# RWKV's chunk inverse: its 16x16 diagonal blocks go to VectorE, through a DRAM scratch

## The reference

```python
def step(S, inp):
    r_t, w_t, k_t, v_t, kk_t, a_t = inp
    sa = jnp.einsum("bhvk,bhk->bhv", S, -kk_t)
    S = (S * w_t[:, :, None, :]
         + sa[..., None] * (kk_t * a_t)[:, :, None, :]
         + v_t[..., None] * k_t[:, :, None, :])
    return S, jnp.einsum("bhvk,bhk->bhv", S, r_t)
```

## Time and profile before

| | |
|---|---|
| three timed runs | 3728.26, 3730.78, 3735.71 us |
| median | 3730.78 us |
| the profiled execution's own time | 3736.72 us |
| its span, first to last instruction | 3734.7 us |
| mixers of both layers | about 60 to 2400 us |
| TensorE, VectorE, ScalarE busy | 95%, 36%, 19% of the span |
| mean granted TensorE clock | 0.97 |

### The profile page before, as it was taken

The page is one execution under the profiler, slowest core; times in us unless marked ns, Lnnn a source line. Parts: engine busy times, 40 slices in busy tenths (PEclk is TensorE's granted clock), DMA queues, the critical chain, the costliest instruction groups (busy, mean ns, idle before and its releaser), DMA issues.

```text
span 3734.7 us, 43111 instructions
## 1 busy us (share of the span) xinstructions
PE 3535.5 (95%) x18508; PEld 2956.0 (79%) x18508; DVE 1335.7 (36%) x2779; ACT 720.5 (19%) x1360; POOL 43.5 (1%) x51
## 2 busy tenths in 40 slices
PE   7997999998999999999999999899989988997999
PEld 6997988998987898898898898686658747855684
DVE  3546546537410463655645531100130012015100
ACT  2223222313100232322313210100010011002100
POOL 0000000000000000000000000000000000000000
PEclk9998999999999999998999999999989989997999
DMA  4112122112124321211212122444434423431343
GB/s 183 57 68 71 68 71 79 57 71 91 68 105 150 121 68 68 94 68 49 80 68 84 67 91 102 142 152 153 147 102 139 154 99 124 147 126 68 113 151 108
DMA packets 53117, 375.55 MB, mean 101 GB/s; under 512 B 6049, under 2 KB 6177, under 8 KB 9025
## 3 DMA queue, kind: packets, MB, share of 16 engines
q1 hardware_dynamic: 51376, 368.01, 28.4%
q0 software_dynamic: 1552, 4.79, 0.4%
HBM read 371.72 MB, written 1.05 MB: 100 GB/s over the span
## 4 chain that ended last, share of the span: by engine, by line
PE 90%; DVE 7%; ACT 1%; issue 1%; DMA 1%; SPq 0%; ACTq 0%; DVEq 0%
PE bank L418 42%; PE bank L1635 11%; PE bank L1572 6%; PE bank L435 5%; PE bank L721 5%; PE bank L743 4%; PE bank L732 4%; PE bank L1194 1%; DVE rw_score L998 1%; PE bank L456 1%; PE bank L660 1%; PE bank L1458 1%; PE bank L772 1%; PE bank L708 1%; PE bank L756 1%
## 5 line engine op out<-in xcount | busy, mean ns | idle before, releaser
L418 PE MATMUL bank<-h_features,weight_ring 128*128 128x256 f32 x7072 | 1594.4, 383 | 16.6 <-DMA weight_ring<-in_w_in 9.7
L418 PEld LDWEIGHTS bank<-h_features,weight_ring 128*128 128x128 f32 x7072 | 1335.0, 191 | 200.8 <-issue 13.5
L1635 PE MATMUL bank<-weight_ring,ff_act 128*128 128x512 f32 x704 | 303.1, 592 | 4.7 <-DVE ff_act L1718 4.7
L1635 PEld LDWEIGHTS bank<-weight_ring,ff_act 128*128 128x128 f32 x704 | 133.4, 190 | 172.7 <-issue 166.5
L1718 DVE TENSOR_TENSOR ff_act<-ff_silu,bank 128x256 f32<-128x256 f32 x88 | 37.1, 421 | 577.2 <-ACT ff_silu L1709 577.2
L721 PE MATMUL bank<-rw_bm,rw_score 128*128 128x64 f32 x1536 | 206.5, 278 | 7.2 <-DVE rw_bm L1023 3.7
L721 PEld LDWEIGHTS bank<-rw_bm,rw_score 128*128 128x128 f32 x1536 | 194.7, 196 | 13.7 <-issue 3.4
L435 PE MATMUL bank<-weight_ring,h_features 128*128 128x256 f32 (+2 forms) x896 | 202.5, 375 | 2.0 <-DVE h_features L501 2.0
L743 PE MATMUL bank<-rw_ex,rw_sig 128*128 128x64 f32 x1536 | 203.6, 276 | 0.0
L1023 DVE COPY_PREDICATED rw_bm<-mask_constants,bank 128x256 f32<-128x256 uint32 x160 | 78.6, 491 | 330.8 <-PE bank L732 330.4
L743 PEld LDWEIGHTS bank<-rw_ex,rw_sig 128*128 128x128 f32 x1536 | 191.6, 194 | 1.4
(11 more groups left out here) (420 smaller groups left out, 3592.3 us busy)
## 6 DMA issues: line engine op xcount, KB each, us to landing
weight_ring<-in_w_in SPq DMA_DIRECT2D x146, 1024.0 KB, 4.9
weight_ring<-in_f00w SPq DMA_DIRECT2D x33, 1024.0 KB, 4.9
weight_ring<-in_f01w SPq DMA_DIRECT2D x33, 1024.0 KB, 4.8
weight_ring<-in_f10w SPq DMA_DIRECT2D x33, 1024.0 KB, 4.9
weight_ring<-in_f11w SPq DMA_DIRECT2D x33, 1024.0 KB, 4.9
weight_ring<-in_w_b SPq DMA_DIRECT2D x16, 1024.0 KB, 5.0
weight_ring<-in_w_out SPq DMA_DIRECT2D x16, 1024.0 KB, 5.2
weight_ring<-in_conv_in SPq DMA_DIRECT2D x10, 1024.0 KB, 4.8
```

What stands on the lines that cost most here:

```text
L418: m = e.matmul(bank[:, j, :], w[:, k, j * P:(j + 1) * P], x[:, k, :], start=k == 0, stop=k == kt - 1, skip_group_check=True)
L1635: m = e.matmul(banks[i], src[:, k0 + k, t * P:(t + 1) * P], w[:, k, s * 512:(s + 1) * 512], start=k0 + k == 0, stop=k0 + k == k_tiles - 1, ...
```

## The change

The levels 2, 4 and 8 of the doubling and the "first" products leave TensorE. In their place a unit does this, for both chunks and all four heads at once:

- TensorE makes the a-scores of both chunks first (four banks, two products each), and VectorE masks them into R.scored_a. The kd-scores follow in each step, into R.scored_k;
- ScalarE's queue stores slot 0 of each chunk in a DRAM scratch (`scratch_rows`: 128 partitions x 4 heads, runs of 512 B), waits, and loads the 64 diagonal blocks of 16x16 back with one block on each of 64 partitions (`scratch_blocks`: 64 blocks x 16 rows, runs of 64 B);
- VectorE inverts them in place (`block_inverse_dve`): 4x4 blocks by substitution, then two doublings by multiply and reduce (`product_dve`), and the transposed copy;
- ScalarE's queue stores the inverse and its transpose in two more scratches, and loads each chunk's x and xT from them before the step's first level. The zeros off the blocks come from the scratches, which POOL clears once at the start (`clear_scratch_pool`).

A chunk has 8 diagonal blocks of a head; two chunks and four heads make the 64. On VectorE's queue the masks of scored_k stand behind the inverse. The loads of step 1 are issued when w of step 0 is done, behind ScalarE's copies of tok. The orders of both mixer layers are written anew for TensorE, VectorE, ScalarE and SP. The masks first0 and first1 are gone from the constants.

```diff
     ("mixers0", "tensor"):
-        "H2 R20 H2 R5 H12 R9 H R3 H R4 H R4 H3 R4 B R3 B H R B R3 B R2 H2 R2 B R2 B R4 H2 R8 B R3 B2 R3 H2 R3 B R "
...
+        "H2 R20 H2 R5 H12 R6 H6 B4 R2 B3 R H R3 B2 R B R5 H2 R2 B R2 B R4 H2 R4 B2 R3 B R4 H2 R3 B R2 B R2 H2 R2 "
...
-RW_LEVELS = (2, 4, 8, 16, 32, 64)
+RW_LEVELS = (16, 32, 64)
+BLOCK = 16
+HEAD_STRIDE = P // BLOCK * (BLOCK * P + BLOCK)
...
     R.state = R("state", 2, P)
-    R.score = R("score", 4, 4, P)
+    R.scored_a, R.scored_k = R("scored_a", TT, 4, 2, P), R("scored_k", 4, 2, P)
     R.tot, R.mid, R.phi = R("tot", 4), R("mid", 4), R("phi", 2)
     R.mean, R.var = R("mean", 8), R("var", 8)
     R.prod, R.x, R.xT = (z.rearrange("p n (c s) -> p (n c) s", c=TT) for z in (R.sig, R.bm, R.ex))
+    blocks = TT * 4 * P // BLOCK
+    R.blk, R.inv, R.inv_mid, R.inv_tmp = (flat(z)[0:blocks, a:b] for z, a, b in (
+        (R.sig, 0, 272), (R.bm, 0, 272), (R.bm, 272, 336), (R.ex, 0, 512)))
...
+def scratch_rows(t, c):
+    heads = t[c * 4 * HEAD_STRIDE:(c + 1) * 4 * HEAD_STRIDE].rearrange("(h z) -> h z", h=4)
+    return heads[:, 0:P * P].rearrange("h (s t) -> s h t", s=P)
+def scratch_blocks(t):
+    step = BLOCK * P + BLOCK
+    return t.rearrange("(n z) -> n z", z=step)[:, 0:BLOCK * P].rearrange("n (s t) -> n s t", s=BLOCK)[:, :, 0:BLOCK]
+def block_rows(z):
+    return z[:, 0:BLOCK * BLOCK].rearrange("p (s t) -> p s t", s=BLOCK)
+def diagonal(z, n):
+    step = n * BLOCK + n
+    return z[:, 0:BLOCK // n * step].rearrange("p (b z) -> p b z", z=step)[:, :, 0:n * BLOCK].rearrange(
+        "p b (s t) -> p b s t", s=n)[:, :, :, 0:n]
+def product_dve(e, S, tmp, left, right, outs):
+    dve, n = S.dve, left[0].shape[1]
+    w = tmp[:, 0:len(left) * n ** 3].rearrange("p (b c t k) -> p b c t k", b=len(left), c=n, t=n)
+    for b, (x, y) in enumerate(zip(left, right)):
+        shape = [x.shape[0], n, n, n]
+        e.tensor_tensor(w[:, b], x.rearrange("p k t -> p t k").unsqueeze(1).to_broadcast(shape),
+                        y.unsqueeze(2).to_broadcast(shape), ALU.mult).then_inc(*dve.up())
+    e.wait_ge(*dve.now())
+    for b, out in enumerate(outs):
+        e.tensor_reduce(out, w[:, b], AX.X, ALU.add).then_inc(*dve.up())
+    e.wait_ge(*dve.now())
+def block_inverse_dve(e, g, l, q, d):
+    S, R = g.rw, g.R
+    dve, blk, inv, tmp, mid = S.dve, R.blk, R.inv, R.inv_tmp, R.inv_mid
+    e.memset(inv[:, 0:BLOCK * BLOCK], 0.0).then_inc(*dve.up())
+    e.wait_ge(*dve.now())
+    e.memset(inv[:, 0:BLOCK * BLOCK].rearrange("p (s t) -> p s t", s=BLOCK)[:, 0:1, 0:1], 1.0).then_inc(*dve.up())
+    e.memset(inv[:, 17:17 * BLOCK].rearrange("p (s z) -> p s z", z=17)[:, :, 0:1], 1.0).then_inc(*dve.up())
+    yield
+    e.wait_ge(g.rw_blocks_sem, 16 * ((4 * l + q) * 2 + d + 1))
+    e.wait_ge(*dve.now())
+    b4, i4 = diagonal(blk, 4), diagonal(inv, 4)
+    first, second = (0, 1) if d == 0 else (3, 2)
+    e.tensor_copy(i4[:, :, first, second:second + 1], b4[:, :, first, second:second + 1]).then_inc(*dve.up())
+    e.wait_ge(*dve.now())
+    for i in (2, 3):
+        t, lo = (i, 0) if d == 0 else (3 - i, 4 - i)
+        rows = slice(lo, lo + i)
+        shape = [blk.shape[0], 4, i, i]
+        w = tmp[:, 0:4 * i * i].rearrange("p (b c s) -> p b c s", b=4, c=i)
+        e.tensor_tensor(w, b4[:, :, rows, t].unsqueeze(2).to_broadcast(shape), i4[:, :, rows, rows], ALU.mult
+                        ).then_inc(*dve.up())
+        e.wait_ge(*dve.now())
+        e.tensor_reduce(i4[:, :, rows, t], w, AX.X, ALU.add).then_inc(*dve.up())
+        e.wait_ge(*dve.now())
+    for n in (4, 8):
+        lo, hi = (slice(0, n), slice(n, 2 * n)) if d == 0 else (slice(n, 2 * n), slice(0, n))
+        pairs_of = range(BLOCK // (2 * n))
+        b, x = diagonal(blk, 2 * n), diagonal(inv, 2 * n)
+        m = [mid[:, i * n * n:(i + 1) * n * n].rearrange("p (c k) -> p c k", c=n) for i in pairs_of]
+        product_dve(e, S, tmp, [b[:, i, lo, hi] for i in pairs_of], [x[:, i, lo, lo] for i in pairs_of], m)
+        product_dve(e, S, tmp, [x[:, i, hi, hi] for i in pairs_of], m, [x[:, i, lo, hi] for i in pairs_of])
+    e.tensor_copy(block_rows(tmp), block_rows(inv).rearrange("p c t -> p t c")).then_inc(*dve.up("inverse", l, q, d))
...
+            for c in (0, 1) if d == 0 else (1, 0):
+                for par in range(2):
+                    yield
+                    rows = slice(64 * par, 64 * par + 64)
+                    bank = pairs(g.banks.take(S, "scored_a", l, q, d, c, par))
+                    for free in g.banks.free("scored_a", l, q, d, c, par):
+                        e.wait_ge(*free)
+                    if par == 0:
+                        e.wait_ge(*dve.at("ops", l, q, d))
+                    for n in range(2):
+                        m = e.matmul(bank[:, n, :], R.a[rows, n, c * P:(c + 1) * P],
+                                     R.kr[rows, n, c, :, :].rearrange("p s t -> p (s t)"), start=True, stop=True,
+                                     skip_group_check=True)
+                    m.then_inc(*pe.up("scored_a", l, q, d, c, par))
+
             for step, c in enumerate((0, 1) if d == 0 else (1, 0)):
                 W = (l, q, d, step)
                 cs = slice(c * P, (c + 1) * P)
-                for h in range(4):
-                    n, rows = h // 2, slice(64 * (h % 2), 64 * (h % 2) + 64)
-                    pair = R.kr[rows, n, c, :, :].rearrange("p s t -> p (s t)")
-                    yield
-                    bank = g.banks.take(S, "score", *W, h)
-                    for free in g.banks.free("score", *W, h):
-                        e.wait_ge(*free)
-                    if h == 0:
-                        e.wait_ge(*dve.at("ops", l, q, d))
-                    e.matmul(bank[:, 0:T], R.a[rows, n, cs], pair, start=True, stop=True, skip_group_check=True)
-                    e.matmul(bank[:, T:2 * T], R.kd[rows, n, cs], pair, start=True, stop=True,
-                             skip_group_check=True).then_inc(*pe.up("score", *W, h))
-                    if h % 2 == 1:
-                        yield
-
                 for par in range(2):
                     yield
                     rows = slice(64 * par, 64 * par + 64)
-                    bank = g.banks.take(S, "first", *W, par)
-                    for free in g.banks.free("first", *W, par):
+                    bank = pairs(g.banks.take(S, "scored_k", *W, par))
+                    for free in g.banks.free("scored_k", *W, par):
                         e.wait_ge(*free)
                     for n in range(2):
-                        m = e.matmul(bank[:, n * P:(n + 1) * P], R.kr[rows, n, c, 0, :], R.a[rows, n, cs], start=True,
-                                     stop=True, skip_group_check=True)
-                    m.then_inc(*pe.up("first", *W, par))
-                yield
+                        m = e.matmul(bank[:, n, :], R.kd[rows, n, cs],
+                                     R.kr[rows, n, c, :, :].rearrange("p s t -> p (s t)"), start=True, stop=True,
+                                     skip_group_check=True)
+                    m.then_inc(*pe.up("scored_k", *W, par))
...
-                    e.wait_ge(*dve.at(*(("xT", *W, 1) if lv == 2 else ("x", *W, lv // 2))))
+                    if lv == BLOCK:
+                        e.wait_ge(g.rw_inverse_sem, 32 * (((4 * l + q) * 2 + d) * 2 + step + 1))
+                    else:
+                        e.wait_ge(*dve.at("x", *W, lv // 2))
...
+            unit = (4 * l + q) * 2 + d
+            for c in (0, 1) if d == 0 else (1, 0):
+                yield
+                e.wait_ge(*dve.at("scored_a", l, q, d, c, 1))
+                if unit:
+                    e.wait_ge(g.rw_blocks_sem, 16 * unit)
+                e.dma_start(scratch_rows(g.scores_scratch, c), R.scored_a[:, c, :, 0, :]).then_inc(g.rw_scores_sem, 16)
+            yield
+            e.wait_ge(g.rw_scores_sem, 32 * (unit + 1))
+            e.dma_start(block_rows(R.blk), scratch_blocks(g.scores_scratch)).then_inc(g.rw_blocks_sem, 16)
+            yield
+            e.wait_ge(*dve.at("inverse", l, q, d))
+            e.wait_ge(g.rw_zeros_sem, 32)
+            if unit:
+                e.wait_ge(g.rw_inverse_sem, 64 * unit)
+            e.dma_start(scratch_blocks(g.x_scratch), block_rows(R.inv_tmp)).then_inc(g.rw_stored_sem, 16)
+            e.dma_start(scratch_blocks(g.xT_scratch), block_rows(R.inv)).then_inc(g.rw_stored_sem, 16)
+
             for step, c in enumerate((0, 1) if d == 0 else (1, 0)):
+                W = (l, q, d, step)
                 yield
-                W = (l, q, d, step)
+                if step == 0:
+                    e.wait_ge(g.rw_stored_sem, 32 * (unit + 1))
+                else:
+                    e.wait_ge(*pe.at("w", l, q, d, 0))
+                e.dma_start(R.x, scratch_rows(g.x_scratch, c)).then_inc(g.rw_inverse_sem, 16)
+                e.dma_start(R.xT, scratch_rows(g.xT_scratch, c)).then_inc(g.rw_inverse_sem, 16)
+                yield
...
```

(70 more changed lines are left out.)

27 lines of the change are left out of this document (16 added, 11 removed), and 100 rows, old and new, of the table ORDER.

## The result

The median of four runs is 3561.69 us (3554.92 to 3565.18), beside 3729.55 us of four runs of the kernel before on the same chip: a ratio of 0.9545, with a 95% interval of 0.9527 to 0.9563. The forecast was 3530 us, the range 3435 to 3790. The profiled execution took 3560.88 us, its span is 3558.8 us, 175.9 less than before; by the prediction's sum it should have been 200.9 less.

The account below looks back on a forecast made before the run. The prediction took TensorE's work to bound the kernel: 3736.7 - 348 (removed work) + 114 (gates) + 5 (step 1) + 2 (zeroing) + 26 (clock) = 3536, with the median 6 us lower: 3530 us; range 3435 to 3790.

Parts of the forecast that it names:

- What leaves TensorE: In the mixers: three levels' matmuls save 303.6 us, the "first" products 38.2 plus 5.9 idle before them, 348 in all.
- Only as long as the fixed order still keeps TensorE fed: In the mixers: condition on work taken off TensorE being worth its full price; no size given.
- Price of a DMA leg: Path's transfers: 1.8 us fixed, 42 ns per KB, and f = 25 ns for each packet, one packet per contiguous piece.
- read-modify-write: Stores of 64 B pieces: if each read and wrote 512 B, 135 us more, about 3675; supports the dear-transfers rival.
- Price of the inverse: VectorE's block inverse: 6.2 us a unit, 99 us over all units, about what VectorE lost.
- Two gates: TensorE waits before step 0's rhs (16.0 us path) and level 16 (10.5): less cover, 114 us idle over two layers.
- Step 1: Loads of x and xT land after 6.4 us against 5.6 to 11.0 us of cover: 5 us in all.
- they are late by the same gaps: Other mixers' work queued behind the path's waits, and TensorE's tokens behind rhs, is late by the gates' gaps.
- Clock: Idle TensorE loses granted clock: four long gaps at 4 us, some ten shorter at 1, 26 us in all.
- Short runs are dear: Rival, chance 0.24: short pieces between SBUF and DRAM cost far more; with f = 70 ns a packet, 3810 us.
- The path is hidden: Rival, chance 0.19: with f = 5 ns a packet most gaps are covered, 3445 us.
- The waits hold H and B as well: Rival, chance 0.09: ScalarE's DMA waits delay the other mixers' streams H and B; 100 us added, 3630 us.

Follow-up runs that it names:

- b_drop: The kernel before with levels 2, 4 and 8, the "first" products and their masks left out and nothing in their place: 3488.34 us.
- a_eye: The kernel after without the DRAM path and the inverse; VectorE writes the identity into x and xT in each step: 3491.12 us.
- a_kfirst: The kernel after with VectorE's two masks of scored_k of step 0 moved ahead of the inverse: 3561.07 us.
- a_both: a_kfirst plus a separate semaphore for each load, so level 16 waits for x alone and the next product for xT: 3554.26 us.
- a_runs: The kernel after with the block load and both inverse stores moving the same bytes in 1 KB pieces, from and to wrong places: 3552.29 us.
- a_pool: The kernel after with the path's DMA issues and their waits moved from ScalarE's queue to GpSimd's, in the same order: 3566.67 us.
- d_early: a_both with VectorE's order changed in units 1 and 4 of each layer, so the inverse comes ahead of some other mixers' steps: 3555.18 us.

## Why the prediction was right, and where it was right by accident

The sign and the range hold, and the forecast was 0.9% low. Its terms against the profiled spans:

| term | forecast | measured | from |
|---|---|---|---|
| matmuls removed | -342 | -292 | busy time, b_drop |
| waits in front of and behind them | -6 | +38 | idle time, b_drop |
| new orders, zeroing | +2 | +4 | a_eye less b_drop |
| gates, step 1, clock | +145 | +74 | after less a_eye |
| sum | -201 | -176 | |

The removed work was worth 50 us less and the waits cost 44 more than forecast, and the path cost 71 less. That these cancel to 25 us is luck, and no step of the prediction foresaw it.

**What leaves TensorE** is the step that failed first: 303.6 us for the three levels, as shares of the groups' busy time. The records of neighbouring groups overlap, and the groups count that twice: 3.16 instead of 2.62 us a level, 96 x 0.54 = 52 us, all of the 50 that were too much. The chain view of the same trace, which I had read for its shares alone, had the right price.

**"Only as long as the fixed order still keeps TensorE fed"** stood in the prediction, without a term. The removed matmuls were themselves cover: in the kernel before VectorE's masks ran beside "first" and the small levels. 38 us of waits came up where nothing had been added (b_drop). The prediction took 6 us of idle time as gone; in their place 25 more came at rhs and 9 at HGRN2's products.

**Price of a DMA leg.** f = 25 ns was too dear. q10 spent 3.3% of 16 x 3558.8 us on 100608 packets, 18.7 ns each for 281 B in the mean; 42 ns per KB of it are data, 7 ns the packet. That a run is a packet was right: the packets are the path's 98304 runs and 16 for each of its 144 DMAs. The legs landed in 2.4 and 2.9 us (forecast 3.3 and 3.6), the stores in 2.5 and 2.7 (5.4 for both), the loads in 3.0 and 3.4 (4.8 for both). By the prediction's own 4.6 us per ns this is 83 us of gates.

The Trainium skill, "DMA: Bandwidth & Descriptors", Specifications, asks for 512 B or more because of a read-modify-write; the prediction made 135 us more of it. The 64 B stores land in 2.5 and 2.7 us beside 1.9 and 2.1 with 1 KB runs, and the whole run is 9.4 us apart: at the price that the prediction gave it the rule does not bite here. The page of the profile counts 389.41 MB read from HBM with runs of 64 B and with runs of 1 KB, 17.8 more than in a_eye, which are the path's own loads; whether that count would hold the reads of a read-modify-write no run shows. The 24 ns a run that the prediction worked out from "VectorE: DVE Perf Modes", section "The three transpose paths" (the Trainium skill as well), are nearer, and still more than twice the 10 ns that the measured price (7 ns and 42 ns per KB) makes of a 64 B run.

**Price of the inverse**: 6.2 us forecast, 6.5 to 6.6 measured from its start to its end.

**Two gates.** The prediction had 54 us at rhs and 60 before level 16 of step 0, with some in every unit at the second. Measured are 40.8 and 18.8. In units 1 and 4, where it had 6.1 and 5.3 us, the second gate is as good as closed: the way's time is waited for at rhs and, in unit 4, at HGRN2's products. The path's own share of the idle time within the way is 50 us of the 114, 5.3 us in unit 1 and 6.2 in unit 4 (forecast 16.7 and 18.6 for both gates); the rest there is idle time that a_eye has too. By the measured price of a run alone it would be some 31 (114 less 83). What filled up in units 1 and 4 is VectorE: the inverse starts 9.3 and 10.8 us behind the last scored_a instead of 7, because steps of the other mixers stand ahead of it (unit 1: a mask that waits for HGRN2's product). In unit 5 it is a DMA: the two stores of the scores, issued behind weight loads, land after 8.2 and 7.5 us in place of 2.4, the block load behind them is issued 9.3 us after the last scored_a, and the inverse starts after 12.3.

**Step 1** had 5 us in the prediction's sum, and 13.7 were measured, all in two waits of unit 3: there both loads take 12.0 to 12.4 us in place of 3.0 and 3.4. The prediction priced every load as if the weight loads weren't there.

The gates are not two, either: a_kfirst took the first away, and its time came up before the retention mixer's products. The prediction's "they are late by the same gaps" was right in this; the step that it didn't take is that the gap belongs to the way, less all work ordered inside it whose operands VectorE can deliver.

**Clock**: 26 us forecast; busy time times (1 - clock) in the mixers went from 43.1 to 62.6 us, 47.9 in a_eye: about 15 to 20, in a figure that differs by 7 between two repeats of a_both. Of the toll of 74 us in the table 55 are idle time and 19 busy time.

**Rivals and signs.** "Short runs are dear" fell with a_runs. (Its side sum of "about 3675" is 3530 + 135 = 3665; it changes nothing.) The prediction named gaps below 50 us in all, or long gaps ended by H's chain, as signs of being wrong. The gaps sum to 59.6 us, and HGRN2's chain ends two of 8.25 us; but these two stand in a_eye as well. "The path is hidden" was nearest on the price of a packet (5 ns), but 71 us of toll are not hidden. "The waits hold H and B as well": HGRN2's wait did rise by 21 us, but it does so without the path (a_eye, 33.9), and freeing ScalarE changed nothing (a_pool). My own theory after the result, 120 us of toll with HGRN2 and the ring in it, fell with a_eye.

What is left open: why d_early's 10 us of idle time gave nothing; and whether work pulled into units 1 and 4 in TensorE's own order would fill them, which was not tried, since VectorE's and ScalarE's orders would have to be written anew with it.

## What to carry to other kernels

Price removed work by the chain of waits, where a group takes the time from its start to the next one's start; the groups' busy times count the overlaps twice, here 342 us in place of 292, 17% too much. Ask of removed work what it had covered: here 38 of 292 us came back with nothing put in its place. Before you put down a wait to the new path, look for it in a run without the path: 28 of the 79 us of idle time within the way were there without it. And when a wait goes away without the time changing, look at the engine that both the old and the new wait end on: it is one way with one length, and only its length, or real work inside it, changes what the engine waits in all. Whether the total time follows is a second question: in d_early it didn't.

## What the runs showed of the hardware that I had not expected

A store of 64 KB from SBUF in 1024 runs of 64 B lands 2.5 to 2.7 us after its issue, one in 1 KB runs after 1.9 to 2.1. The issue itself holds ScalarE's queue longer for short runs: block load and the two stores 0.62, 0.60 and 0.70 us (median), in a_runs 0.48, 0.46 and 0.62; the prediction had 0.4 for each.

The same transfer can be slow when weight loads run. In the chain of the kernel after, a step-1 load issued at 484.05, just behind five 1 MB weight loads, takes 12.28 us in place of 3.4, and TensorE waits 6.75 us for it (the line is in the section on the result):

```profile
484.05 12.28 DMA rw_ex<-xT_scratch
```

The last of the five weight loads lands at 495.40, the two loads of step 1 at 495.69 and 496.33. In a_pool, where GpSimd's queue issues them behind three and four of the five weight loads and not behind all of them, they take 7.7 and 9.4 us and land before the last three weight loads, and TensorE waits 1.5 us. That the loads queue behind the weight loads' packets is what these times suggest; no run took the weight loads away to show it, and in a_pool the queue and the moment of issue changed together.
